# A hybrid gMLP and sliding-window decoder trunk: rests taken earlier, take-ups and two bulk transfers taken later

## What is computed

```python
D_MODEL = 1024; SEQ = 2048; A_WIDTH = 2048; A_GROUPS = 8; CHUNK = 128
def mixer_a(h, w_in, ln_g, ln_b, w_s, b_s, w_out):
    u, v, z = jnp.split(h @ w_in, 3, axis=-1)      # w_in: 1024 x 6144
    u = jax.nn.gelu(u)
    v = layer_norm(jax.nn.gelu(v), ln_g, ln_b)
    ...
    mixed = jnp.einsum("gts,bnsgc->bntgc", ws, vc) + b_s.T[:, :, None]
    y = u * mixed.reshape(B, S, A_WIDTH) * jax.nn.silu(z)
    return y @ w_out                               # w_out: 2048 x 1024
# per layer: h = rms_norm(x, norm) * (1 + scale) + shift;  x = x + gate * mixer(h, ...)
```

## Time and profile before

| | us |
|---|---|
| median of 3 runs (2215.28 to 2223.0) | 2217.31 |
| the profiled execution's own time | 2219.44 |
| its span in the trace | 2217.7 |
| PE busy with matmuls in it | 2150.9 (97%) |
| DVE, POOL, ACT busy | 1440.5, 1195.1, 1095.3 |
| bytes moved, mean rate | 592.89 MB, 267 GB/s |
| value stages of chunks 1, 2, 3, roughly | 420 to 499, 773 to 853, 1129 to 1209 |

### The profile page before, as it was taken

How to read it: one execution, slowest core, us unless ns; L and a number is a source line. 1 busy time by engine, 2 the same in 40 slices (tenths; PEclk the granted TensorE clock), 3 DMA queues, 4 the chain that set the end, 5 groups by cost and what they waited for, 6 DMA issues and landing times.

```text
span 2217.7 us, 29383 instructions
## 1 busy us (share of the span) xinstructions
PE 2150.9 (97%) x10410; PEld 1801.0 (81%) x10410; DVE 1440.5 (65%) x1761; ACT 1095.3 (49%) x2050; POOL 1195.1 (54%) x913
## 2 busy tenths in 40 slices
PE   5999999999999999999999999999999999999998
PEld 4887778788888878888777888887888888888887
DVE  6956548757486864554974673767767657656854
ACT  4334446634545744445653445534545646545653
POOL 3456675845553865544594645441535555454542
PEclk9999999999999999999999999999999999999999
DMA  9888889785558785557877556899686697887654
GB/s 347 307 306 308 312 315 356 231 308 174 196 198 324 285 315 191 200 179 269 314 259 283 181 181 218 323 348 365 244 297 225 253 359 266 280 309 288 206 205 171
DMA packets 244787, 592.89 MB, mean 267 GB/s; under 512 B 20929, under 2 KB 96801, under 8 KB 244257
## 3 DMA queue, kind: packets, MB, share of 16 engines
q1 hardware_dynamic: 241680, 585.71, 73.5%
q10 hardware_dynamic: 2960, 5.30, 0.7%
HBM read 461.96 MB, written 119.54 MB: 262 GB/s over the span
## 4 chain that ended last, share of the span: by engine, by line
PE 75%; DMA 6%; POOL 6%; DVE 5%; ACT 3%; DVEq 2%; POOLq 1%; issue 1%; SPq 1%; ACTq 0%
PE ps L2361 22%; PE ps L2363 22%; PE ps L2362 22%; DMA w_raw<-in_a_w_in 3%; POOL w_lo L1130 3%; PE ps L2566 2%; PE ps L2615 1%; PE ps L2616 1%; POOL cbl L1149 1%; PE ps L2641 1%; DVE acc L1812 1%; ACT w_hi L1364 1%; DMA w_lo<-a_weights_combined 1%; PE ps L2650 1%; DVE yb L2093 1%
## 5 line engine op out<-in xcount | busy, mean ns | idle before, releaser
L1130 POOL TENSOR_TENSOR w_lo<-w_raw,w_hi 128x1024 fp32r<-128x1024 f32 x244 | 650.0, 2682 | 569.6 <-ACT w_hi L1364 569.4
L1364 ACT ACTIVATE w_hi<-w_raw 128x1024 fp32r<-128x1024 f32 x260 | 272.0, 1057 | 418.3 <-DMA w_raw<-in_a_w_in 372.7
L2361 PE MATMUL ps<-h,w_hi 128*128 128x512 f32 x1024 | 403.3, 394 | 9.7 <-POOL w_lo L1130 8.3
L2363 PE MATMUL ps<-h,w_lo 128*128 128x512 f32 x1024 | 398.9, 390 | 0.0
L2362 PE MATMUL ps<-h,w_hi 128*128 128x512 f32 x1024 | 398.7, 389 | 0.0
L2361 PEld LDWEIGHTS ps<-h,w_hi 128*128 128x128 f32 x1024 | 192.2, 188 | 55.3 <-POOL w_lo L1130 14.3
L2363 PEld LDWEIGHTS ps<-h,w_lo 128*128 128x128 f32 x1024 | 192.2, 188 | 40.7
L2362 PEld LDWEIGHTS ps<-h,w_hi 128*128 128x128 f32 x1024 | 192.4, 188 | 38.9 <-issue 0.2
L2361 PE MATMUL ps<-r,w_hi 128*128 128x512 f32 x480 | 191.6, 399 | 1.9 <-issue 1.9
L2363 PE MATMUL ps<-r,w_lo 128*128 128x512 f32 x480 | 187.7, 391 | 0.0
L2362 PE MATMUL ps<-r,w_hi 128*128 128x512 f32 x480 | 187.3, 390 | 0.0
(11 more groups left out here) (277 smaller groups left out, 4902.6 us busy)
## 6 DMA issues: line engine op xcount, KB each, us to landing
w_raw<-in_a_w_in SPq DMA_DIRECT2D x256, 256.0 KB, 3.6
w_hi<-b_weights_split SPq DMA_DIRECT2D x104, 512.0 KB, 4.7
w_lo<-b_weights_split SPq DMA_DIRECT2D x104, 512.0 KB, 6.3
w_raw<-in_a_w_in SPq DMA_DIRECT2D x52, 512.0 KB, 4.7
w_raw<-in_a_w_out SPq DMA_DIRECT2D x48, 512.0 KB, 5.4
w_hi<-v_weights_combined SPq DMA_DIRECT2D x48, 512.0 KB, 3.9
w_lo<-v_weights_combined SPq DMA_DIRECT2D x48, 512.0 KB, 5.2
w_hi<-a_weights_combined SPq DMA_DIRECT2D x32, 512.0 KB, 6.6
```

The source lines that it names most:

```text
L1130: g.tensor_tensor(wlo[p][:, rows_], raw[p][:, rows_], whi[p][:, rows_].bitcast(F32), ALU.subtract).then_inc(w_lo, 1)
L1364: s_.activation(whi[p][:, rows_], raw[p][:, rows_], ACT.Copy).then_inc(w_hi, 1)
L2361: t_.matmul(dst_, stat[0], mov[0], start=start, stop=False)
L2363: return t_.matmul(dst_, stat[1], mov[0], start=False, stop=stop)
```

## The change

It leaves every product and every operand as they are and moves work in time. In the first half of a value stage POOL takes the first rest of s2 before it forms the second three sums, and forms the last two sums (for s3) only after the rests of products 3 to 5; ACT rounds weight unit 3 between the roundings of s2, s1 and s4, and rounds s3 after weight unit 5. DVE waits for three sums, not for eight, before product 2's result, for which `uu` moves to another 4 KB of the arena. The take-ups `out_late` 4 and 5 follow product 6 of the first half. SP issues the store of x1 after unit 11 and a split load, not after unit 9, and in the output stage issues `keep_turned` and `load_x` after unit 5, not after unit 4.

```diff
@@ -503,7 +503,7 @@
         tabs = place("tabs", gt + 12 * K, [T], F32)
 
         ut, ue = place("ut", hfx_at, [2, T], F32), place("ue", xst_at, [2, T], F32)
-        uu = place("uu", y_at + 16 * K, [2, T], F32)
+        uu = place("uu", y_at + 24 * K, [2, T], F32)
 
         up = place("up", cs_at, [2, T], F32)
 
@@ -987,7 +987,6 @@
                         unit(v_unit(i, n))
                         if n == 11:
                             load_split(split_at(i, 3))
-                        if n == 9:
                             sp.wait_ge(ao_read, at("ao_read", i - 1, 8))
                             for cnk in range(NC):
                                 sp.dma_start(x1d[i - 1, :, cnk], x1[:, cnk, :]).then_inc(x1_out, 16)
@@ -999,9 +998,9 @@
                     if i == 0 and n == 15:
                         combs_kept(0)
                     unit(ao_first(i) + n)
-                    if i >= 1 and n == 4:
+                    if i >= 1 and n == 5:
                         keep_turned(i - 1, GROUPS - 1)
-                    if i < NG - 1 and n == 4:
+                    if i < NG - 1 and n == 5:
                         load_x(i + 1)
                     if n == 7:
                         load_residual(i)
@@ -1169,8 +1168,8 @@
                 pool.drain()
                 s_add(2, q, h_block(0, 1, q), ALU.subtract, s_whole(0, q))
 
-            def s_rest(i, s):
-                for q in range(2):
+            def s_rest(i, s, halves=(0, 1)):
+                for q in halves:
                     there = S_ORDER[s][:, 2 * q:2 * q + 2]
                     pool.wait_ge(s_hi, s_parts(i, s, q))
                     g.tensor_tensor(there[:, :, 1, :], s_whole(s, q), there[:, :, 0, :].bitcast(F32),
@@ -1210,15 +1209,16 @@
                     pool.wait_ge(piece_done, PIECES_BY[FIRST[i]])
                     pool.wait_ge(xt_full, at("xt_full", i, 8))
                     s_sums(0)
+                    s_rest(i, 0, (0,))
                     pool.wait_ge(h_hi, at("h_hi", i, 8))
                     s_sums(1)
-                    s_rest(i, 0)
-                    for q in range(2):
-                        s_add(3, q, h_block(0, 0, q), ALU.subtract, h_block(1, 0, q))
+                    s_rest(i, 0, (1,))
                     lo(v_unit(i, 3))
                     s_rest(i, 1)
                     s_rest(i, 2)
                     lo(v_unit(i, 5))
+                    for q in range(2):
+                        s_add(3, q, h_block(0, 0, q), ALU.subtract, h_block(1, 0, q))
                     s_rest(i, 3)
                     lo(v_unit(i, 7))
                     lo(v_unit(i, 10))
@@ -1501,14 +1501,16 @@
                         s_.activation(ut[:, c, :], bank(2 * sv + c), ACT.Copy).then_inc(first_kept, 1)
                     if sv == 0:
                         s_round(i, 0, (1,))
+                        hi(v_unit(i, 3), (0,))
                         s_round(i, 1)
+                        hi(v_unit(i, 3), (1,))
                         s_round(i, 2)
-                    hi(v_unit(i, 7 * sv + 3))
-                    if sv == 0:
+                        hi(v_unit(i, 5))
                         s_round(i, 3)
                     else:
+                        hi(v_unit(i, 10))
                         x1_squares(i - 1)
-                    hi(v_unit(i, 7 * sv + 5))
+                        hi(v_unit(i, 12))
                     for c in range(2):
                         gelu(sv, c, 2 * sv, 7 + c)
                     hi(v_unit(i, 7) if sv == 0 else uz_unit(i, 0, 0))
@@ -1989,7 +1991,7 @@
                         out_late(i - 1, 1)
                     if sv == 0:
 
-                        dve.wait_ge(s_sum, 8 * i)
+                        dve.wait_ge(s_sum, 8 * (i - 1) + 3)
                     block_out(sv, 2, (flat(uu), flat(ut)), (flat(ue), flat(ue)))
                     if late:
                         out_late(i - 1, 2)
@@ -1997,16 +1999,15 @@
                     if late:
                         out_late(i - 1, 3)
                     block_out(sv, 4, (flat(uu), flat(uu)))
-                    if late:
-                        out_late(i - 1, 4)
                     for c in range(2):
                         v_stat(j, c, 8 * sv + c + 1)
                     block_out(sv, 5, (lambda c: v_chunk(j + 1, c), flat(uu)))
-                    if late:
-                        out_late(i - 1, 5)
                     for c in range(2):
                         v_stat(j + 1, c, 8 * sv + c + 3)
                     block_out(sv, 6, (lambda c: v_chunk(j + 1, 2 + c), flat(uu)), (lambda c: v_chunk(j, 2 + c), flat(ue)))
+                    if late:
+                        out_late(i - 1, 4)
+                        out_late(i - 1, 5)
 
                 def last_stats(sv):
                     for c in range(2):
```

## The result

The changed kernel takes **2222.45 us** (median of 12 runs, 2218.93 to 2229.15) against 2217.28 for the kernel before in runs beside it (12 runs, 2213.96 to 2223.0): ratio **1.0024, 95% interval 1.0016 to 1.0032**. That is 5.2 us slower where 6.8 faster was forecast, and outside the range. By the bound of 0.3% it is no change, but the interval lies above 1. The profiled execution has a span of 2224.8 us.

A forecast was written before the change was run, and what follows sets the result against it. PE, busy 97% of the span, was taken as the bound, so only its waits or half-clock time could be won. Terms 4.6 + 3.8 - 1.8 + 1.0 - 0.8 = 6.8 us, from 2217.3 to 2210.5; range 2205.5 to 2215.5.

The forecast's parts named there:

- First half: Value stage, products 2 and 3: POOL's new order removes six PE stops, winning 4.6 us, low end 1.8.
- the rival that "issue" at product 2 is PE's own: Value stage, product 2: three stops of 0.92 us stay, 4.0 us won in all, 2213.3 us; chance 0.08.
- Unit 10: Value stage, second half: with the store of x1 behind unit 11, all three stops at unit 10 go, winning 3.8 us.
- Unit 12: Value stage, second half: unit 12 comes late, with new stops costing 1.0, 0.2 and 0.6 us, 1.8 given back.
- upper end of 3.8: Unit 12's term at its largest loss, 3.8 us, if unit 12 is as late as unit 10 was.
- The first rival: Unit 12 takes unit 10's place: 3.8 us given back in full, 4.8 won, 2212.5 us; chance 0.18.
- Output stages: Later x load: 1.0 us won in chunk 2, 0.8 lost in chunk 1 through later (3,0), 0 in chunk 0.
- Chunk 2's gain of 1.5 + 1.7: Output unit (2,1): stop 1.5 us shorter and no clock fall, 1.7 more; of this 3.2, 1.0 was kept.
- Chunk 0: 0: Output stage of chunk 0: no cost from the late x load, as nothing is kept and ACT is as late.
- the rival that starves: Output units (3,0), (3,1): weights reach ACT over 3 us later; 11.3 us lost overall, 2228.6 us; chance 0.06.
- The take-ups: Value stage, take-ups 4 and 5: moved to where POOL is idle, they cost nothing.
- partial overlap: Output stage: POOL's four rests and DVE's operand rests ran on together, each slowed; an exclusive lock would make chunk 2 keep 0.

The follow-up runs named there:

- e7: Kernel before plus the first half's new order, with the four stores of x1 behind the eight units of the first u/z group: 2209.51 us, ratio 0.9957.
- e9: Kernel before plus the first half's new order, with one store of x1 behind each of units 9 to 12: 2208.43 us, ratio 0.9956.
- e1: Kernel before with the first-half part alone (POOL's and ACT's order, DVE's wait, place of `uu`): 2211.21 us, ratio 0.9973.
- e13: Kernel before, unchanged, in another profiled execution: chunk 2's stop at output unit (2,1) was 0.83 us instead of 2.10.
- e3: Kernel before with `load_x` and `keep_turned` alone issued after unit (2,1) instead of (2,0): 2221.05 us, ratio 1.0012.
- e2: Kernel before with the store of x1 alone moved behind unit 11 and the split load: 2227.49 us, ratio 1.0044.
- e4: Whole change without its late `load_x` and `keep_turned`, against the kernel before: 2220.26 us, ratio 1.0013.
- e11: Kernel before with take-ups 4 and 5 alone moved behind product 6: 2220.14 us, ratio 1.0009.

## Why the prediction was wrong

**First half: right.** 4.6 forecast, 4.9 in the profile, 6 as run alone (interval 4 to 8). POOL's order decides; the rival that "issue" at product 2 is PE's own has fallen.

**Unit 10: right.** The three stops went, 4.0 for 3.8, and with the stores placed so that unit 12 doesn't suffer, e7 and e9 lie 0.17% below e1, 3.7 us (the intervals overlap). But e13 shows that the stops of the earlier trace rows are only one form of that loss: where the first take-up lasts 7.7 us, in chunks 1 and 2 of that execution, PE stops at product 7 and not at unit 10. And in e1's profile, with the stores in their old place, unit 10 stops PE in chunk 3 alone, for 1.38. In chunk 1 it lands there 7.5 us after its issue behind the same four stores, not 10.2. So how much the stores' new place wins at unit 10 differs between executions, and 4.0 is a large case of it.

**Unit 12: the failed step.** The sentence is "The queue is never quite empty in between, so I place it at 482.3". Units 10 and 11 now find an empty queue, are served at once, and leave it dry while SP waits to issue the next. Counted from PE's end of unit 9, unit 12 should have landed 1.8 + 482.3 - 476.04 = 8.1 us later (the working has PE win 1.8 ahead of that point) and landed 486.41 - 476.96 = 9.5 later. That makes 0.75 of stop into 2.15. Two slips in the term are small beside this: the first half's own sum gives 4.6 / 3 = 1.5 for that 1.8 (measured 1.6), and chunk 2's 0.2 should be 0.75 - 0.44 + 0.24, some 0.6. The rest of the term's error is what it left out: the same text prices the fall of the clock after a 2.10 us stop at 1.7 us in chunk 2, and gives none to unit 12, whose upper end of 3.8 had stops of a microsecond. With 2.1 for each stop and two falls it is 10.3 of the 10.5 measured. Stops of over 1 us at unit 12 in all three chunks were among the prediction's own signs of being wrong. The first rival named this place and the stores ahead of it, at 3.8, but not the dry queue, which the text looked for only in the output stages.

**Output stages.** Chunk 2's gain of 1.5 + 1.7 was read from a stop that was chance, so nothing stood against the loss: set against e13, the change loses 0.6 us in chunk 2. The loss itself was taken too small. In chunk 1 (3,0) was to land some 3 us later and landed at 726.2 instead of 717.6, which is 5.2 later when PE's own 3.4 are taken off. "Chunk 0: 0" was 1.9, but that is not all the x load's. It is mostly 1.0 lost at (5,0) with POOL first, and 1.1 at a new stop at (2,1). e7, with the x load in its old place, shows both in chunk 0 (its stop at (2,1) is 0.56), and e3, with the late x load, doesn't have the one at (2,1). The text also misread the stop at (3,1) as the end of all four of POOL's rests: PE goes on at 731.12, the third ends at 730.98 and the fourth at 733.33. The sign of the rival that starves was right for (3,0), its size not: as run alone the part costs 2.7 us, not 5 to 16.

**The take-ups** cost nothing within the whole change, as far as the runs can tell: e1 and e2 add up to +0.17%, and e4, which has both and the take-ups, is at +0.13%. In the rows on POOL's four rests the prediction saw "partial overlap". The exclusive lock of which the Trainium skill speaks (SBUF — State Buffer, section "SBUF: two separate sides") fits them better than that reading did: 12.41 us for four rests are 4 x 2.39 and 2.9 more, because three of them take 3.4, a microsecond more each, with one of DVE's operations of 1.2 beside each. In the changed kernel, where DVE waited for ACT over most of them, the same four took 10.47. That did not decide the result.

In sum: forecast 6.8 won. With 10.5 for 1.8 at unit 12, nothing in chunk 2 and 4.1 lost in chunks 0 and 1, the same working gives 4.9 + 4.0 - 10.5 - 4.1 = 5.7 lost, where 5.2 was measured. The terms are those of single executions, so an agreement this close is partly luck.

## What to carry to other kernels

A large transfer that isn't urgent delays what stands behind it in the queue, and moving it in one piece only moves the victim. Put it in pieces where the queue would otherwise run dry, and check both ends: which unit is behind each piece, and which engine waits, in order, for the last one. Before a stop in one profiled execution is priced as a gain, see whether a second execution of the same kernel has it: here one of some 3 us was in one profile and in none of the seven others with the x load in that place, a second one of the same kernel among them.

## What the hardware showed

**A DVE operation can lose to POOL several times in a row.** The take-up of 0.69 us reads two operands from SBUF. In e13 it started at 449.25, beside four operations of POOL that ran back to back from 449.17 to 456.4, and ended at 456.97, half a microsecond after the last of them. In the other execution of the same kernel it got in after 1.77 us, and POOL's pairs took 3.02 and 5.21 us instead of 2.55 and 4.77. Over the nine profiled executions that have the take-ups in their old place, three chunks each, it took from 0.9 to 7.8 us; behind product 6 always 0.69. The Trainium skill, SBUF — State Buffer, section "SBUF: two separate sides", says that the port pair of DVE and GpSimd is an exclusive lock, held for a whole instruction by whichever starts first. The rows agree with the lock, and show that the loser may not be next in line. At POOL's four rests of an output stage the two do take turns, and there a start of 0.05 us ahead by POOL decides whether DVE's first operation takes 1.2 or 3.3 us ("The x load spread").

**The clock doesn't follow from the stop alone.** After stops of 2.15 and 2.10 us at unit 12 the granted clock fell to 1.2 GHz for a while, after one of 2.12 in chunk 2 it did not. With e2 and e4 there are nine such stops, of 2.1 to 2.5 us: six with a fall and three without (2.12, 2.38 and 2.19), while one of 1.86 in e11 was followed by a fall.
